# First mixture of experts: the weight splitting issued in pairs of pieces, six split slots, and a new order on ScalarE

## The chip, the core and the metric

The kernel runs on one core of a Trainium2 chip. The metric is the device time in microseconds (us) of one execution; the kernel before takes 2359.21 us, the median of 3 runs (2356.23 to 2360.47). Engines are named as the profile names them: PE is TensorE's matmul, PEld its weight load, DVE is VectorE, ACT is ScalarE, SP is the engine that issues the DMAs.

## The reference, cut to what matters

The program is a transformer block with a mixture of experts, followed by two more layers (a dense feed-forward in one, a second mixture in the other). All is float32, on 256 tokens of width 1024. The change is written in the first mixture, 16 experts, of which each token uses two:

```python
y = jnp.zeros_like(t)
for e in range(N_EXPERTS):
    he = jax.nn.silu(t @ w_gate[e]) * (t @ w_up[e])
    y = y + combine[:, e:e + 1] * (he @ w_down[e])
```

`w_gate` and `w_up` are 1024 x 512 for each expert, `w_down` is 512 x 1024: 6.29 MB of weights per expert, and no weight is read twice.

## The kernel before, in words

**Pieces.** All weights pass through one stream of numbered pieces of 128 x 1024 elements (0.5 MB). SP loads two at a time into `ring`, which has 12 slots (`RAW`). ScalarE copies a piece into `ring_hi`, rounded to the type that TensorE multiplies fast (`make_hi`, L421), and VectorE writes what the rounding lost into `ring_lo` (`make_lo`, L426). Both have 4 slots (`FINE`). TensorE multiplies with both parts and counts each piece it is done with on the semaphore `used` (called `pieces_used` on the chip).

**What holds what back.** `make_hi` of piece n waits until the piece has arrived and until `used` is at least n + 1 - FINE: the slot that it overwrites must be free. `make_lo` waits for the high part. A slot of `ring` is free for the next load when its low part is written.

**First mixture.** `stacked_experts` handles it, one expert per turn i of a loop that is written out 16 times. Expert i has 4 gate pieces, 4 up pieces, and in the same turn come the 4 down pieces of expert i - 1; in the stream their order is gate(i), up(i), down(i-1). TensorE's order in turn i is: gate(i) (L1506, L1507, 16 matmuls); turning the return table and folding the rows of expert i - 1 (L1543, L1554); up(i) (16 matmuls); a part of the gathering of later tokens (L1464); the scatter of four earlier experts into one quarter of the output (L1523); down(i-1) (16 matmuls). ScalarE's order and VectorE's order are in the two blocks below. ScalarE also copies gate rows (L1632), up rows (L1612), the return table (L1604, L1606), the gathered tokens (L1475, `xg`), the SiLU (L1616), the high part of the hidden rows (L1620), and the expert's output (L1600, `copy_output`). VectorE multiplies SiLU and up (L1662), makes the low part of the hidden rows (L1666), the low part of the output (L1671, `low_output`) and adds the scattered quarter to x (L1678, `add_to_x`).

**Second mixture.** 8 experts in 7 chunks each, by `sparse_experts`, with the same `make_hi`, `make_lo` and slots. Each piece is multiplied three ways (L442 to L444), so TensorE has 6 matmuls per piece. Once per expert, at its first chunk, the finished expert's output is scattered (L1240) and VectorE adds it to x in two instructions (L1375); TensorE may start the next down pieces only when both are done, since they go to the same banks. In VectorE's order these two stand behind the low parts of the first two down pieces, and those behind four up pieces, the low part of the output (`y_lo`, L1353), and four gate pieces.

Of the kernel before, what the change touches and what calls it, by code (L numbers as in the profile page):

```python
# [19 lines left out]
F32 = mybir.dt.float32  # L20
F32R = mybir.dt.float32r
BF16 = mybir.dt.bfloat16
ALU = mybir.AluOpType
ACT = mybir.ActivationFunctionType
# [118 lines left out]
class WeightStream:  # L143
# [1 line left out]

    RAW, FINE, AHEAD = 12, 4, 2

    def __init__(self):  # L150
        self.items, self.count = [], 0
# [14 lines left out]
def build(nc, ctx, A, consts_dram, const_cols, out):  # L166
# [29 lines left out]
    v, sc, pe = nc.vector, nc.scalar, nc.tensor  # L196
# [12 lines left out]
    ring = sb("ring", [P, WeightStream.RAW, 1024])  # L209
    ring_hi = sb("ring_hi", [P, WeightStream.FINE, 1024], dtype=F32R)  # L210
    ring_lo = sb("ring_lo", [P, WeightStream.FINE, 1024], dtype=F32R)
    x = sb("x", [P, HALVES, D])
# [12 lines left out]
    def bank(b, n=1):  # L225
        return psum[:, b * BANK:(b + n) * BANK]
# [170 lines left out]
    def raw_view(buf, slots, num, a, width):  # L397
        return buf[:, num[0] % slots, 0:a * width].rearrange("p (a n) -> p a n", a=a)
# [18 lines left out]
    def make_hi(e, num, a=2, width=FF):  # L417
        e.wait_ge(arrived[num[0] % RAW // 2], num[1] * 16 + 16 * (num[0] // RAW + 1))
        if not (isinstance(num[1], int) and num[0] + 12 * num[1] < FINE):
            e.wait_ge(used, count_after(num, 1 - FINE))  # L420
        sc.activation(raw_view(ring_hi, FINE, num, a, width), raw_view(ring, RAW, num, a, width), ACT.Copy) \  # L421
            .then_inc(hi_ready, 1)

    def make_lo(e, num, a=2, width=FF):
        e.wait_ge(hi_ready, count_after(num))
        v.tensor_tensor(raw_view(ring_lo, FINE, num, a, width), raw_view(ring, RAW, num, a, width),  # L426
                        raw_view(ring_hi, FINE, num, a, width).bitcast(F32), ALU.subtract).then_inc(lo_ready, 1)

    def make_his(e, pcs):
        for p in pcs:  # L430
# [964 lines left out]
    def stacked_experts(group, xn_split, disp, tag):  # L1395
# [15 lines left out]
        def gate_piece(i, q):  # L1411
            return group.n0 + q if i == 0 else group.n0 - 4 + 12 * i + q

        def up_piece(i, q):
            return gate_piece(i, q) + 4

        def down_piece(ex, j):
            return group.n0 + 16 + 12 * ex + j if ex < E - 1 else group.n0 - 4 + 12 * E + j

        def gathers(i):  # L1420
            return i + 1 < E
# [16 lines left out]
        def programs(st):  # L1438
# [157 lines left out]
            def scalar(e):  # L1596
                def copy_output(ex):
                    e.wait_ge(used, down_piece(ex, 3) + 1)
                    e.wait_ge(ret_ok, ex + 1)
                    sc.activation(y[0][ex % WIN], bank(3, 2), ACT.Copy, scale=weights[:, ex % WIN:ex % WIN + 1]).then_inc(y_out, 1)  # L1600

                def copy_return(ex):
                    e.wait_ge(ret_t, ex + 1)
                    sc.activation(both_sums[:], weight_sums(ex), ACT.Copy,  # L1604
                                  accum_out=weights[:, ex % WIN:ex % WIN + 1])
                    sc.copy(retT[:, ex % COPIES, :], bank(6)[:, E:E + SEQ]).then_inc(ret_ok, 1)  # L1606

                def copy_up(ex):
                    e.wait_ge(used, up_piece(ex, 3) + 1)
                    if ex:  # L1610
                        e.wait_ge(folded, ex)
                    sc.copy(u_sb[:], bank(1)).then_inc(u_out, 1)  # L1612

                def silu_of(ex):
                    e.wait_ge(folded, ex + 1)
                    sc.activation(s_g[:], gT, ACT.Silu).then_inc(silu, 1)  # L1616

                def high_hidden(ex):
                    e.wait_ge(hid, ex + 1)
                    sc.copy(hT[:, :, 0:SLOTS], hidden[:]).then_inc(hid_hi, 1)  # L1620

                for i in range(E):
                    for q in range(group.early if i == 0 else 0, 4):
                        make_hi(e, (gate_piece(i, q), 0))
                    if i > 1:
                        copy_output(i - 2)
                    for q in range(4):
                        make_hi(e, (up_piece(i, q), 0))
                    e.wait_ge(used, gate_piece(i, 3) + 1)
                    if i:  # L1630
                        e.wait_ge(folded, i)
                    sc.copy(g_sb[:], bank(0)).then_inc(g_out, 1)  # L1632
                    if i:
                        copy_return(i - 1)
                        silu_of(i - 1)
                        make_hi(e, (down_piece(i - 1, 0), 0), 1, 1024)
                        high_hidden(i - 1)
                        for j in range(1, 4):
                            make_hi(e, (down_piece(i - 1, j), 0), 1, 1024)
                    if gathers(i):  # L1640
                        for n in range(2):
                            first = min(i + 1, E - WIN)
                            e.wait_ge(gathered, 2 * i + n + 1)
                            copy_gathered(sc.copy, 2 * (i % 4) + n, first, bank(6 + n)).then_inc(xg_ok, 1)
                    copy_up(i)
                copy_output(E - 2)
                copy_return(E - 1)
                silu_of(E - 1)
                make_hi(e, (down_piece(E - 1, 0), 0), 1, 1024)
                high_hidden(E - 1)  # L1650
                for j in range(1, 4):
                    make_hi(e, (down_piece(E - 1, j), 0), 1, 1024)
                copy_output(E - 1)
                make_his(e, group.next)
                sc.preload_act_table_set(LOG_EXP)

            def vector(e):
# [20 lines left out]
                    v.tensor_tensor(to, to, bank(b), ALU.add).then_inc(added, 1)  # L1678

                for i in range(E):  # L1680
                    for q in range(group.early if i == 0 else 0, 4):
                        make_lo(e, (gate_piece(i, q), 0))
                    if i > 1:
                        low_output(i - 2)
                    if i > 2:
                        add_to_x(i - 3, scatter_plan[i - 1][0], 5)
                    for q in range(4):
                        make_lo(e, (up_piece(i, q), 0))
                    if i:
                        hidden_of(i - 1)  # L1690
                        make_lo(e, (down_piece(i - 1, 0), 0), 1, 1024)
                        low_hidden(i - 1)
                        for j in range(1, 4):
                            make_lo(e, (down_piece(i - 1, j), 0), 1, 1024)
                low_output(E - 2)
                add_to_x(E - 3, scatter_plan[E - 1][0], 5)
                hidden_of(E - 1)
                make_lo(e, (down_piece(E - 1, 0), 0), 1, 1024)
                low_hidden(E - 1)
                for j in range(1, 4):  # L1700
                    make_lo(e, (down_piece(E - 1, j), 0), 1, 1024)
                low_output(E - 1)
                for quarter in range(QUARTERS):
                    e.wait_ge(added, E - 2)
# [2013 lines left out]
```

## Time and profile before

| | |
|---|---|
| median of 3 runs | 2359.21 us |
| the profiled execution's own time | 2364.25 us |
| its span | 2362.1 us |
| busy PE / DVE / ACT | 95% / 78% / 65% |
| moved by DMA | 593.67 MB |
| first mixture, from its first to its last weight matmul | 290.7 to 574.8 us |
| second mixture | about 1322 to 2330 us |

A matmul of 512 columns is shown as about 390 ns, but the next one starts about 227 ns after it: matmuls are pipelined, and starts are what counts. The same holds for the instructions of DVE and ACT, which overlap by a little.

### The profile page before, as it was taken

How to read it: one execution, taken by the hardware profiler on the slowest of the kernel's cores; microseconds unless marked ns; L12 is line 12 of the kernel's file. 1: busy time of each engine (PE TensorE's matmuls, PEld its weight loads, DVE VectorE, ACT ScalarE, POOL GpSimd, SP SyncE). 2: the span in 40 equal slices, each digit the busy share in tenths (PEclk: the TensorE clock that was granted, in tenths of full speed). 3: DMA queues.
4: the chain of work that ended last, by engine and by line, in shares of the span. 5: the costliest groups of instructions: out<-in, count | busy, mean ns of one | idle time of the engine just before them, and what ended most of it. 6: DMA issues, size and time to landing. Idle time of an engine off the chain costs nothing. (4 is left out here: it accounts for less than half of the span.)

```text
span 2362.1 us, 35287 instructions
## 1 busy us (share of the span) xinstructions
PE 2242.1 (95%) x12323; PEld 1839.0 (78%) x12323; DVE 1846.9 (78%) x2017; ACT 1539.5 (65%) x2045; POOL 45.4 (2%) x56
## 2 busy tenths in 40 slices
PE   7989889999998999999989899999999999999997
PEld 6778567776776799987767688888888888888886
DVE  4655689997657656566667799999999999999995
ACT  4554389896544544455544587877777777777785
POOL 0000000000002000000003000000000000000000
PEclk9989999999989999999989999999999999999999
DMA  8434099997530355555500599999999999999892
GB/s 311 147 107 143 35 356 369 367 368 281 179 130 2 130 180 178 195 172 178 185 1 25 226 377 347 359 348 358 348 362 349 354 355 352 353 356 373 335 377 84
DMA packets 93735, 593.67 MB, mean 251 GB/s; under 512 B 17312, under 2 KB 20288, under 8 KB 22592
## 3 DMA queue, kind: packets, MB, share of 16 engines
q1 hardware_dynamic: 93632, 592.30, 67.1%
q8 instruction: 65, 1.06, 0.2%
q14 instruction: 38, 0.31, 0.0%
HBM read 591.21 MB, written 1.05 MB: 251 GB/s over the span
## 5 line engine op out<-in xcount | busy, mean ns | idle before, releaser
L426 DVE TENSOR_TENSOR ring_lo<-ring,ring_hi 128x1024 fp32r<-128x1024 f32 (+1 forms) x1120 | 1337.4, 1216 | 276.9 <-ACT ring_hi L421 215.9
L421 ACT ACTIVATE ring_hi<-ring 128x1024 fp32r<-128x1024 f32 (+1 forms) x1120 | 1162.5, 1056 | 410.8 <-PE psum L444 389.3
L442 PE MATMUL psum<-ring_hi,xg_hi 128*128 128x512 f32 x896 | 354.3, 395 | 3.7 <-DVE ring_lo L426 2.4
L444 PE MATMUL psum<-ring_hi,xg_lo 128*128 128x512 f32 x896 | 349.6, 390 | 0.0
L443 PE MATMUL psum<-ring_lo,xg_hi 128*128 128x512 f32 x896 | 348.9, 389 | 0.0
L442 PE MATMUL psum<-ring_hi,xT_hi 128*128 128x512 f32 (+2 forms) x512 | 200.7, 392 | 14.0 <-DVE ring_lo L426 6.1
L442 PEld LDWEIGHTS psum<-ring_hi,xg_hi 128*128 128x128 f32 x896 | 168.3, 188 | 37.7 <-DVE ring_lo L426 2.9
L443 PE MATMUL psum<-ring_lo,xT_hi 128*128 128x512 f32 (+2 forms) x512 | 197.3, 385 | 0.0
L444 PE MATMUL psum<-ring_hi,xT_lo 128*128 128x512 f32 (+2 forms) x512 | 197.1, 385 | 0.0
L444 PEld LDWEIGHTS psum<-ring_hi,xg_lo 128*128 128x128 f32 x896 | 168.2, 188 | 35.7
L443 PEld LDWEIGHTS psum<-ring_lo,xg_hi 128*128 128x128 f32 x896 | 168.5, 188 | 33.4
L442 PE MATMUL psum<-ring_hi,hT_hi 128*128 128x512 f32 x448 | 176.1, 393 | 8.0 <-DVE x L1375 5.6
L444 PE MATMUL psum<-ring_hi,hT_lo 128*128 128x512 f32 x448 | 174.5, 390 | 0.0
L443 PE MATMUL psum<-ring_lo,hT_hi 128*128 128x512 f32 x448 | 174.4, 389 | 0.0
L442 PE MATMUL psum<-xT_hi,ring_hi 128*128 128x256 f32 x480 | 136.1, 284 | 2.6 <-DVE xT_lo L1838 1.6
L444 PE MATMUL psum<-xT_hi,ring_lo 128*128 128x256 f32 x480 | 135.9, 283 | 0.0
L443 PE MATMUL psum<-xT_lo,ring_hi 128*128 128x256 f32 x480 | 135.9, 283 | 0.0
L442 PEld LDWEIGHTS psum<-ring_hi,xT_hi 128*128 128x128 f32 x512 | 98.3, 192 | 36.4 <-issue 9.2
L1506 PE MATMUL psum<-ring_hi,xg 128*128 128x512 f32 x256 | 112.7, 440 | 8.6 <-DVE ring_lo L426 6.4
L444 PEld LDWEIGHTS psum<-ring_hi,xT_lo 128*128 128x128 f32 x512 | 98.3, 192 | 19.3
L443 PEld LDWEIGHTS psum<-ring_lo,xT_hi 128*128 128x128 f32 x512 | 98.5, 192 | 17.8
L442 PEld LDWEIGHTS psum<-ring_hi,hT_hi 128*128 128x128 f32 x448 | 84.1, 188 | 28.4 <-issue 9.6
(549 smaller groups left out, 3227.8 us busy)
## 6 DMA issues: line engine op xcount, KB each, us to landing
ring<-in_moe_w_gate_dram SPq DMA_DIRECT2D x112, 1024.0 KB, 4.8
ring<-in_moe_w_up_dram SPq DMA_DIRECT2D x112, 1024.0 KB, 4.8
ring<-in_moe_w_down_dram SPq DMA_DIRECT2D x112, 1024.0 KB, 4.7
ring<-in_w_in_dram SPq DMA_DIRECT2D x38, 1024.0 KB, 5.6
ring<-in_w_gate_dram SPq DMA_DIRECT2D x32, 1024.0 KB, 6.9
ring<-in_w_up_dram SPq DMA_DIRECT2D x32, 1024.0 KB, 7.2
ring<-in_w_down_dram SPq DMA_DIRECT2D x32, 1024.0 KB, 7.1
ring<-in_ffn_w_gate_dram SPq DMA_DIRECT2D x14, 1024.0 KB, 4.8
```

The costliest lines, as they stand in the source:

```text
L421: sc.activation(raw_view(ring_hi, FINE, num, a, width), raw_view(ring, RAW, num, a, width), ACT.Copy) \
L426: v.tensor_tensor(raw_view(ring_lo, FINE, num, a, width), raw_view(ring, RAW, num, a, width), raw_view(ring_hi, FINE, num, a, width).bitca ...
L442: pe.matmul(out_, lhsT[0], rhs[0], start=start, stop=False)
L443: pe.matmul(out_, lhsT[0], rhs[1], start=False, stop=False)
L444: return pe.matmul(out_, lhsT[1], rhs[0], start=False, stop=stop)
L1506: pe.matmul(to, lhsT, w[0], start=start, stop=False)
```

## The change

Five things are changed. `FINE` goes from 4 to 6, for the whole program. In the first mixture `make_hi` and `make_lo` are replaced by versions that treat two pieces in one instruction of 2048 columns; the high version waits for `used` to be at least n + 2 - FINE, where n is the first piece of the pair, the low one for both high parts. On ScalarE the four gate pieces of expert i + 1 are moved from the head of turn i + 1 to turn i: the first pair ahead of the token copies, the second between them and the copy of the up rows. The first pair of down pieces moves ahead of the copy of the gate rows. And the size of a scratch buffer is set to 1024 bytes, which makes room for the two more slots.

```diff
-    RAW, FINE, AHEAD = 12, 4, 2
+    RAW, FINE, AHEAD = 12, 6, 2
...
+    def pair_view(buf, slots, n):
+
+        return buf[:, n % slots:n % slots + 2, :].rearrange("p m x -> p (m x)")
+
+    def make_hi_pair(e, n):
+        e.wait_ge(arrived[n % RAW // 2], 16 * (n // RAW + 1))
+        e.wait_ge(used, n + 2 - FINE)
+        sc.activation(pair_view(ring_hi, FINE, n), pair_view(ring, RAW, n), ACT.Copy).then_inc(hi_ready, 2)
+
+    def make_lo_pair(e, n):
+        e.wait_ge(hi_ready, n + 2)
+        v.tensor_tensor(pair_view(ring_lo, FINE, n), pair_view(ring, RAW, n), pair_view(ring_hi, FINE, n).bitcast(F32),
+                        ALU.subtract).then_inc(lo_ready, 2)
...
+                for q in range(group.early, 4, 2):
+                    make_hi_pair(e, gate_piece(0, q))
                 for i in range(E):
-                    for q in range(group.early if i == 0 else 0, 4):
-                        make_hi(e, (gate_piece(i, q), 0))
                     if i > 1:
                         copy_output(i - 2)
-                    for q in range(4):
-                        make_hi(e, (up_piece(i, q), 0))
+                    for q in range(0, 4, 2):
+                        make_hi_pair(e, up_piece(i, q))
+                    if i:
+                        make_hi_pair(e, down_piece(i - 1, 0))
                     e.wait_ge(used, gate_piece(i, 3) + 1)
...
                     if i:
                         copy_return(i - 1)
                         silu_of(i - 1)
-                        make_hi(e, (down_piece(i - 1, 0), 0), 1, 1024)
                         high_hidden(i - 1)
-                        for j in range(1, 4):
-                            make_hi(e, (down_piece(i - 1, j), 0), 1, 1024)
+                        make_hi_pair(e, down_piece(i - 1, 2))
                     if gathers(i):
+                        make_hi_pair(e, gate_piece(i + 1, 0))
                         for n in range(2):
...
                             copy_gathered(sc.copy, 2 * (i % 4) + n, first, bank(6 + n)).then_inc(xg_ok, 1)
+                        make_hi_pair(e, gate_piece(i + 1, 2))
                     copy_up(i)
...
-    nc = _bacc.Bacc("TRN2", target_bir_lowering=False, num_devices=1)
+    nc = _bacc.Bacc("TRN2", target_bir_lowering=False, num_devices=1,
+                    dynamic_dma_scratch_size=1024)
```

On VectorE the loops over single pieces become loops over pairs; the order is kept. Line numbers of the changed kernel are 14 to 16 higher there (`make_hi_pair` is L436, `make_lo_pair` L440).

ScalarE in the first mixture, before, from one expert's output copy to the gate pieces of the next expert (`L421` is `make_hi`, `L1475` the token copies, `L1612` the up rows):

```order
L1600 ACTIVATE y_rows<-psum,slot_weights 128x1024
L421 ACTIVATE ring_hi<-ring 128x1024 x4
L1632 COPY gate_rows<-psum 128x512
L1604 ACTIVATE weight_parts,slot_weights<-psum 128x2
L1606 CAST return_pT<-psum 128x256
L1616 ACTIVATE silu_gT<-psum 128x256
L421 ACTIVATE ring_hi<-ring 128x1024
L1620 CAST hT<-hiddenT 128x4x64
L421 ACTIVATE ring_hi<-ring 128x1024 x3
L1475 CAST xg<-psum 128x2x4x64 x2
L1612 COPY up_rows<-psum 128x512
L421 ACTIVATE ring_hi<-ring 128x1024 x4
```

The same stretch of ScalarE in the changed kernel (`L436` is `make_hi_pair`, `L1489` the token copies, `L1626` the up rows):

```order
L1614 ACTIVATE y_rows<-psum,slot_weights 128x1024
L436 ACTIVATE ring_hi<-ring 128x2048 x3
L1648 COPY gate_rows<-psum 128x512
L1618 ACTIVATE weight_parts,slot_weights<-psum 128x2
L1620 CAST return_pT<-psum 128x256
L1630 ACTIVATE silu_gT<-psum 128x256
L1634 CAST hT<-hiddenT 128x4x64
L436 ACTIVATE ring_hi<-ring 128x2048 x2
L1489 CAST xg<-psum 128x2x4x64 x2
L436 ACTIVATE ring_hi<-ring 128x2048
L1626 COPY up_rows<-psum 128x512
```

The group of three is up, up, down; of the group of two the second is the first gate pair of the next expert, and the single one after the token copies is its second gate pair. In the kernel before all four gate pieces of the next expert stand behind the up rows.

VectorE in the first mixture, before, one turn from the low part of an output to the next gate pieces:

```order
L1671 SCALAR_TENSOR_TENSOR xT_lo<-psum,slot_weights,y_rows 128x1024
L1678 TENSOR_TENSOR x<-x,psum 128x512
L426 TENSOR_TENSOR ring_lo<-ring,ring_hi 128x1024 x4
L1662 TENSOR_TENSOR hiddenT<-silu_gT,psum 128x256
L426 TENSOR_TENSOR ring_lo<-ring,ring_hi 128x1024
L1666 TENSOR_TENSOR hT<-hiddenT,hT 128x4x64
L426 TENSOR_TENSOR ring_lo<-ring,ring_hi 128x1024 x7
```

The same turn of VectorE in the changed kernel:

```order
L1686 SCALAR_TENSOR_TENSOR xT_lo<-psum,slot_weights,y_rows 128x1024
L1693 TENSOR_TENSOR x<-x,psum 128x512
L440 TENSOR_TENSOR ring_lo<-ring,ring_hi 128x2048 x2
L1677 TENSOR_TENSOR hiddenT<-silu_gT,psum 128x256
L440 TENSOR_TENSOR ring_lo<-ring,ring_hi 128x2048
L1681 TENSOR_TENSOR hT<-hiddenT,hT 128x4x64
L440 TENSOR_TENSOR ring_lo<-ring,ring_hi 128x2048 x3
```

Nothing changes place on VectorE but one thing: the low part of the second down piece is now made together with the first, ahead of the low part of the hidden rows. TensorE's order and that of the DMA issues are the same as before.

## Rows read from the trace of the kernel before

**Rows 1.** Windows: stretch, length, busy by engine, PE clock, DMA share, GB/s.

```profile
375.00:545.00 170.00, 170.00 (x837) 131.89 (x836) 161.10 (x160) 155.13 (x229) 0.00 (x0) 1.00 0.96 369
1380.00:2322.00 942.00, 933.10 (x4327) 773.88 (x4325) 870.14 (x804) 735.10 (x765) 0.00 (x0) 1.00 0.92 353
```

**Rows 2.** Timeline, DVE, one turn: start, length, engine, line, operation, count.

```profile
424.44 4.63 DVE L426 TENSOR_TENSOR ring_lo<-ring,ring_hi 128x1024 fp32r<-128x1024 f32 x4 [0.87 <-ACT ring_hi L421]
...
430.78 4.62 DVE L426 TENSOR_TENSOR ring_lo<-ring,ring_hi 128x1024 fp32r<-128x1024 f32 x4
...
437.17 3.50 DVE L426 TENSOR_TENSOR ring_lo<-ring,ring_hi 128x1024 fp32r<-128x1024 f32 x3
441.58 1.23 DVE L426 TENSOR_TENSOR ring_lo<-ring,ring_hi 128x1024 fp32r<-128x1024 f32 x1 [0.92 <-ACT ring_hi L421]
```

**Rows 3.** Timeline, ACT, the same turn.

```profile
435.77 0.41 ACT L1620 CAST hT<-hiddenT 128x256 fp32r<-128x256 f32 x1 [0.89 <-DVE hiddenT L1662]
436.08 2.95 ACT L421 ACTIVATE ring_hi<-ring 128x1024 fp32r<-128x1024 f32 x3
438.94 1.17 ACT L1475 CAST xg<-psum 128x384 fp32r<-128x384 f32 x4
439.98 0.62 ACT L1612 COPY up_rows<-psum 128x512 f32<-128x512 f32 x1
440.46 1.10 ACT L421 ACTIVATE ring_hi<-ring 128x1024 fp32r<-128x1024 f32 x1
```

**Rows 4.** Waits, 300 to 550 us: total, times, longest.

```profile
PEld psum L1506 <- DVE ring_lo L426: 24.0, 69, 0.4
DVE ring_lo L426 <- ACT ring_hi L421: 18.1, 18, 4.4
```

**Rows 5.** Groups by shape, 276 to 281 us: busy, mean ns.

```profile
L3459 DVE TENSOR_TENSOR xn_moe_lo<-xn_rows,xn_moe_hi 128x2048 fp32r<-128x2048 f32 x1 | 2.3, 2293 | 0.8 <-DVEq L193 0.8
L3454 ACT CAST xn_moe_hi<-xn_rows 128x2048 fp32r<-128x2048 f32 x1 | 1.9, 1881 | 0.0
```

**Rows 6.** Timeline, PE, one turn, and the start of expert 1.

```profile
304.32 0.77 PE L1506 MATMUL psum<-ring_hi,xg 128*128 128x512 f32 x1 [3.61 <-DVE ring_lo L426]
...
430.16 0.65 PE L1543 MATMUL psum<-consts,dispatch 128*128 128x144 f32 x4
...
432.35 0.48 PE L1506 MATMUL psum<-ring_hi,xg 128*128 128x512 f32 x1
...
439.27 0.39 PE L1506 MATMUL psum<-ring_hi,hT 128*128 128x512 f32 x1
...
442.68 0.39 PE L1507 MATMUL psum<-ring_lo,hT 128*128 128x512 f32 x1
...
444.00 0.50 PE L1506 MATMUL psum<-ring_hi,xg 128*128 128x512 f32 x1
444.33 0.40 PE L1507 MATMUL psum<-ring_lo,xg 128*128 128x512 f32 x1
```

**Rows 7.** Timeline, second mixture, ACT, DVE and PE where an expert changes.

```profile
1461.35 1.01 ACT L1299 ACTIVATE y_hi<-psum 128x1024 fp32r<-128x1024 f32 x1
...
1462.83 1.22 DVE L1353 TENSOR_TENSOR y_lo<-psum,y_hi 128x1024 fp32r<-128x1024 f32 x1
...
1471.48 1.28 DVE L1375 SCALAR_TENSOR_TENSOR x<-psum,comb,x 128x1024 f32<-128x1024 f32 x1
1473.07 1.28 DVE L1375 SCALAR_TENSOR_TENSOR x<-psum,comb,x 128x1024 f32<-128x1024 f32 x1 [0.31 <-DVE x L1375]
...
1473.35 0.39 PE L444 MATMUL psum<-ring_hi,xg_lo 128*128 128x512 f32 x1
1474.48 0.49 PE L442 MATMUL psum<-ring_hi,hT_hi 128*128 128x512 f32 x1 [0.75 <-DVE x L1375]
```

**Rows 8.** Waits of PE, whole span.

```profile
PE psum L442 <- DVE ring_lo L426: 11.7, 8, 4.3
PE psum L442 <- DVE x L1375: 5.6, 7, 1.2
```

More of the change, by code:

```diff
@@ L1648, in scalar @@
                 silu_of(E - 1)
-                make_hi(e, (down_piece(E - 1, 0), 0), 1, 1024)
+                make_hi_pair(e, down_piece(E - 1, 0))
                 high_hidden(E - 1)
-                for j in range(1, 4):
-                    make_hi(e, (down_piece(E - 1, j), 0), 1, 1024)
+                make_hi_pair(e, down_piece(E - 1, 2))
                 copy_output(E - 1)
@@ L1680, in vector @@
                 for i in range(E):
-                    for q in range(group.early if i == 0 else 0, 4):
-                        make_lo(e, (gate_piece(i, q), 0))
+                    for q in range(group.early if i == 0 else 0, 4, 2):
+                        make_lo_pair(e, gate_piece(i, q))
                     if i > 1:
@@ L1686, in vector @@
                         add_to_x(i - 3, scatter_plan[i - 1][0], 5)
-                    for q in range(4):
-                        make_lo(e, (up_piece(i, q), 0))
+                    for q in range(0, 4, 2):
+                        make_lo_pair(e, up_piece(i, q))
                     if i:
                         hidden_of(i - 1)
-                        make_lo(e, (down_piece(i - 1, 0), 0), 1, 1024)
+                        make_lo_pair(e, down_piece(i - 1, 0))
                         low_hidden(i - 1)
-                        for j in range(1, 4):
-                            make_lo(e, (down_piece(i - 1, j), 0), 1, 1024)
+                        make_lo_pair(e, down_piece(i - 1, 2))
                 low_output(E - 2)
@@ L1697, in vector @@
                 hidden_of(E - 1)
-                make_lo(e, (down_piece(E - 1, 0), 0), 1, 1024)
+                make_lo_pair(e, down_piece(E - 1, 0))
                 low_hidden(E - 1)
-                for j in range(1, 4):
-                    make_lo(e, (down_piece(E - 1, j), 0), 1, 1024)
+                make_lo_pair(e, down_piece(E - 1, 2))
                 low_output(E - 1)
```

## The prediction

> **What bounds the kernel now.** I read the page's slices first, to find the stretches where DMA and the engines are busiest, then windows for each stage, then the timeline of one turn engine by engine, and the waits last. The reader should see three things.
>
> First, in the first mixture nobody has much room. TensorE is shown busy throughout, VectorE 161.10 of 170 us, ScalarE 155.13, and DMA stands at a share of 0.96 [rows 1]. One expert takes 441.58 - 424.44 = 17.14 us [rows 2]. VectorE idles once a turn, 0.9 us, and waits there for ScalarE's high part of the next expert's first gate piece [rows 2]. ScalarE is late with it because it does the high parts of three down pieces, the token copies and the up rows first, back to back from 436.08 [rows 3]. So the turn is a ring of ScalarE and VectorE: the hidden rows on VectorE release ScalarE at 435.77, and 440.46 + 1.10 = 441.56 releases VectorE again. TensorE waits in small bits for low parts, 69 times, 24.0 us as PEld counts them [rows 4].
>
> Second, the second mixture is bound by TensorE (933.10 of 942 us, DMA share 0.92) [rows 1]. What TensorE loses there is the wait for the addition to x, 7 times, 5.6 us in all [rows 8].
>
> Third, outside the mixtures TensorE's waits for low parts come to 11.7 us over the whole span, the longest 4.3 [rows 8].
>
> **The change part by part, first mixture.** Pairs save the fixed part of an instruction. Low parts of single pieces start (4.63 - 1.23) / 3 = 1.13 us apart [rows 2]; an instruction of 2048 columns of the same kind takes 2.29 us alone [rows 5], less the overlap of 0.1 that the singles show (1.23 - 1.13) it is 2.19 a pair. That is 0.07 a pair, about 0.45 us a turn on VectorE. On ScalarE singles start (2.95 - 1.10) / 2 = 0.925 apart [rows 3] and a pair takes 1.88, 1.78 after overlap [rows 5]: 0.07 a pair, again 0.45 a turn. With the idle time gone VectorE alone would turn in 17.14 - 0.92 - 0.45 = 15.8 us. DMA, at a share of 0.96 now, would be full at 17.14 x 0.96 = 16.5.
>
> But a pair asks for two free slots. The second gate pair of expert i + 1 must wait until `used` reaches n - 4, and counted back through the stream that is the second down piece of turn i. It is a new chain, and it runs through all three engines. With P the start of TensorE's first down matmul:
> - two down pieces, 8 matmuls 0.227 apart ((442.68 - 439.27) / 15) and 0.39 for the last: 7 x 0.227 + 0.39 = 1.98 [rows 6];
> - ScalarE's pair 1.88 and VectorE's pair 2.29 [rows 5], and three handoffs at 0.04 (441.58 comes 0.02 after ScalarE's end [rows 2, 3]), 0.12: TensorE gets the second gate pair at P + 6.27, while it would be ready for it at about P + 5.6 (24 matmuls and one restart);
> - gate pieces 2 and 3: 8 matmuls, the first step 0.33 after a wait (444.33 - 444.00), 1.94; then turning and folding 432.35 - 430.16 = 2.19 [rows 6]: the up matmuls start at P + 10.4;
> - from the first up matmul to the next P the trace has 439.27 - 432.35 = 6.92, with two small waits in it [rows 6]. With pairs only one wait can be there: the second up pair is written at 6.23 + 1.71 (from the end of the gate parts, 424.44 + 4.63, to 430.78) + 2.19 + 2.29 = P + 12.4 [rows 2, 5], and TensorE wants it at P + 12.3. I take 6.8.
>
> Sum: 6.27 + 4.13 + 6.8 = 17.2 us a turn, against 17.14. The stall of VectorE moves from the first gate piece to the second gate pair and grows to about 1.4 us, which eats what the pairs save. ScalarE meets its other dates: the first gate pair needs all up pieces used (about P + 14.6) and is ready by P + 17, before VectorE wants it at P + 17.5. So the 12 turns in the steady state are worth +0.06 x 12 = +0.7. Without the small up wait the turn is 17.0 (-2 over the 12); with handoffs of 0.1 and a full 6.92 it is 17.5 (+4).
>
> The first turns are not steady. TensorE waits 3.61 us for expert 1's gate pieces today [rows 6]. The first pair of them now comes early, but the second still stands behind the token copies, and expert 0's up pieces come in pairs, one step of 1.1 later. I walked these turns the same way and find TensorE 2 us ahead by the fourth. Bounds: all 3.6 of that wait, or 1 us lost (the coarser step alone). Taken: -2. The last turns keep their order. First mixture together: -1, between -6 and +5.
>
> **Six slots elsewhere.** ScalarE may now be two more pieces ahead of TensorE. In a steady TensorE-bound stage that is worth nothing. It is worth something where VectorE falls behind for a moment: where an expert of the second mixture changes. There VectorE's order is four gate parts, `y_lo`, four up parts, the low hidden rows, two down parts, then the two additions. The second addition ends at 1473.07 + 1.28 = 1474.35, and TensorE, whose matmul before started at 1473.35, would have gone on at 1473.58: it restarts at 1474.48 with a step longer by 0.1, so 1.0 us are lost [rows 7]. What holds VectorE back is how late it enters this passage, since until then each low part follows a high part that waits for a slot. With two pieces more, of 6 matmuls each, it would be up to 12 x 0.227 = 2.7 us ahead, except that `y_hi` on ScalarE has to wait for the last down piece: it starts at 1461.35 because another high part stands before it, and could start at 1460.4 [rows 7]. That puts `y_lo` at 1461.45 instead of 1462.83, the additions 1.0 us or more earlier, and TensorE no longer waits. The first of the 7 waits (the longest, 1.2 [rows 8]) comes where VectorE is held by something else, and stays. Gain: 5.6 - 1.2 = 4.4, and 6 x 0.1 for restarts, 5.0. Bounds: 0 (the additions come no earlier) and 6.3 (all seven).
>
> Of the 11.7 us of waits for low parts [rows 8] the longest, 4.3, is set by the order of the code, not by slots: ScalarE and VectorE do a norm there before more pieces. (The wait of 3.6 us counted above is under another line of the matmuls and not among them.) What I can tie to slots is where low parts waited for high parts that waited for TensorE in the two input projections. Taken: -2, between 0 and -5. The scratch size costs nothing: no queue but SP's moves this kernel's data.
>
> Sum: -1 - 5 - 2 = -8. The profiled execution took 2364.25 (span 2362.1), 5.0 above the median of the runs; 2364.25 - 8 = 2356.2 in its terms, 2351 in those of the runs.
>
> **The rivals.**
> - A: the new chain does not close, VectorE turns at its own pace and DMA sets the end at 16.5 us a turn. For it: VectorE's one idle wait today [rows 4] is the one that the new order removes. Against it: `used` needs the second down piece, as counted above. It gives 12 x (17.2 - 16.5) = 8 more: 2343. The Trainium skill speaks for this case (VectorE: DVE Perf Modes, the section on the TRN2 errata): the latency of SBUF is paid between instructions, so fewer and larger ones are faster. By that rule alone the mixture gains; the trace has the same saving, but VectorE's time is not what closes my chain.
> - B: nothing comes of the slots. The additions to x are still late, for VectorE is busy without a gap from the gate parts on, and the first mixture is even. For it: the first of the seven waits is of that kind. It gives -1 to -2: 2358.
> - C, slower: TensorE's one wait of 0.7 us and more in each turn, in place of many small ones, lets its clock fall. Place: the second gate pair. For it: after the wait of 3.61 us the next matmul took 0.77 us instead of 0.39, as at the lower of the clock's two levels, 1.2 against 2.4 GHz [rows 6]. Against it: waits of 0.75 in the second mixture are followed by 0.49 and then full speed [rows 7], at a granted clock of 1.00 [rows 1]. If it happens, and the 8 matmuls of the two gate pieces then take a step of 0.454 instead of 0.227, that is 1.8 us for each of 12 turns, 22, less 8 of the forecast's gains: 2359 + 14 = 2373. It decides from 0.7 us lost a turn, where 12 x 0.7 outweighs those 8. The chain at its long end, 17.5, falls short of that point by itself.
>
> **How the numbers follow.** Forecast 0.55 (its own range 2346 to 2356), A 0.15, B 0.19, C 0.11. Below 0.2% (4.7 us) this measurement can't tell a change from none. Faster than 2354.5: nine tenths of the forecast less the weak end of its bounds, say 0.44, and A, 0.15, together 0.59. Same: the rest of the forecast, 0.11, B, 0.18, together 0.29. Slower: C and a little of B, 0.12. The range reaches from A's lower side, 2341, to 2362, just beyond B, and leaves C out.
>
> **What would show it.** In the changed profile the turn of the first mixture is 17.0 to 17.4 us; VectorE waits once a turn, before the second gate pair, for ScalarE, which itself waits there for TensorE's down matmuls; TensorE has one wait of about 0.7 us between the second and third gate piece. If instead VectorE has no such wait and the turn is near 16.5 with a DMA share of 1, A is right. In the second mixture the waits for the addition to x should be 1 or 2 instead of 7; 7 again is B. Matmuls twice as long inside the steady turns are C. I am wrong altogether if the turn is longer than 17.5 at full clock, or if a stage that I gave nothing moves by more than 3 us.

## The result, and the profile after

| | before | after |
|---|---|---|
| median | 2359.21 us | 2346.76 us (2341.73 to 2348.26, 5 runs) |
| ratio | | 0.9937, 95% interval 0.9919 to 0.9955 |
| profiled execution, its span | 2364.25, 2362.1 us | 2341.73, 2339.6 us |

The change is worth 12.4 us; a second run of it on another chip gave 0.9938 (0.9924 to 0.9951). The forecast was 2351, 8 us faster. But the gain doesn't come from the first mixture, for which most of the change is written.

Windows of the changed kernel, the stretches that answer to [rows 1] (columns as there; the second is shifted by 10 us, since the second mixture starts earlier):

```profile
375.00:545.00 170.00, 161.40 (x819) 132.57 (x818) 153.61 (x98) 148.13 (x165) 0.00 (x0) 1.00 0.96 364
1370.00:2312.00 942.00, 935.31 (x4340) 777.73 (x4339) 840.67 (x810) 715.01 (x774) 0.00 (x0) 1.00 0.92 350
```

In the first mixture TensorE is now busy 161.40 of 170 us, where it was 170.00, and less is moved per second, 364 GB/s against 369. In the second mixture it is busy for 2.2 us more in the same length: more of the work lies in the window.

VectorE, one turn of the changed kernel, from one second gate pair to the next:

```profile
418.17 2.29 DVE L440 TENSOR_TENSOR ring_lo<-ring,ring_hi 128x2048 fp32r<-128x2048 f32 x1 [1.64 <-ACT ring_hi L436]
...
429.44 4.49 DVE L440 TENSOR_TENSOR ring_lo<-ring,ring_hi 128x2048 fp32r<-128x2048 f32 x2
435.57 2.29 DVE L440 TENSOR_TENSOR ring_lo<-ring,ring_hi 128x2048 fp32r<-128x2048 f32 x1 [1.64 <-ACT ring_hi L436]
```

435.57 - 418.17 = 17.40 us a turn, against 17.14 [rows 2]. The idle time of 0.92 us before the first gate piece has become one of 1.64 before the second gate pair. ScalarE in the same turn says why:

```profile
427.02 0.41 ACT L1634 CAST hT<-hiddenT 128x256 fp32r<-128x256 f32 x1 [0.78 <-DVE hiddenT L1677]
427.33 3.72 ACT L436 ACTIVATE ring_hi<-ring 128x2048 fp32r<-128x2048 f32 x2
430.96 1.17 ACT L1489 CAST xg<-psum 128x384 fp32r<-128x384 f32 x4
433.55 1.92 ACT L436 ACTIVATE ring_hi<-ring 128x2048 fp32r<-128x2048 f32 x1 [1.43 <-PE psum L1521]
435.37 0.57 ACT L1626 COPY up_rows<-psum 128x512 f32<-128x512 f32 x1
```

It is no longer late with its own work, as in [rows 3]: it stands idle for 1.43 us behind the token copies and waits for TensorE (`PE psum L1521`, a weight matmul) to be done with a slot. TensorE, from the first down matmul to the next turn's:

```profile
431.45 0.39 PE L1520 MATMUL psum<-ring_hi,hT 128*128 128x512 f32 x1
...
436.67 0.39 PE L1521 MATMUL psum<-ring_lo,xg 128*128 128x512 f32 x1
437.92 0.50 PE L1520 MATMUL psum<-ring_hi,xg 128*128 128x512 f32 x1 [0.86 <-DVE ring_lo L440]
438.25 0.39 PE L1521 MATMUL psum<-ring_lo,xg 128*128 128x512 f32 x1
...
442.06 0.48 PE L1520 MATMUL psum<-ring_hi,xg 128*128 128x512 f32 x1
...
448.85 0.39 PE L1520 MATMUL psum<-ring_hi,hT 128*128 128x512 f32 x1
```

So the loop is closed: with P = 431.45, ScalarE starts the pair at P + 2.10, VectorE at P + 4.12, TensorE at P + 6.47. The waits of the stretch 300 to 550 us, next to [rows 4]:

```profile
PEld psum L1520 <- DVE ring_lo L440: 24.9, 29, 2.5
DVE ring_lo L440 <- ACT ring_hi L436: 21.3, 14, 2.7
ACT ring_hi L436 <- PE psum L1521: 18.1, 13, 1.7
```

About as much is waited on low parts, 24.9 us against 24.0, but in 29 pieces, not 69. The third row is the chain's: ScalarE waits for TensorE 13 times, once a turn, where the same wait of the kernel before (`ACT ring_hi L421 <- PE psum L1507`) came 3 times and to 2.0 us.

The pairs themselves are as long as [rows 5] had it, by the groups of the page (busy, mean ns, idle before):

```profile
L440 DVE TENSOR_TENSOR ring_lo<-ring,ring_hi 128x2048 fp32r<-128x2048 f32 x95 | 214.7, 2289 | 31.1 <-ACT ring_hi L436 31.0
L436 ACT ACTIVATE ring_hi<-ring 128x2048 fp32r<-128x2048 f32 x95 | 176.9, 1913 | 19.4 <-PE psum L1521 18.1
```

In the second mixture the timeline where an expert changes answers to [rows 7], ScalarE, VectorE and TensorE:

```profile
1444.63 1.03 ACT L1313 ACTIVATE y_hi<-psum 128x1024 fp32r<-128x1024 f32 x1 [1.66 <-PE psum L458]
```

```profile
1445.69 1.22 DVE L1367 TENSOR_TENSOR y_lo<-psum,y_hi 128x1024 fp32r<-128x1024 f32 x1
...
1456.29 1.28 DVE L1389 SCALAR_TENSOR_TENSOR x<-psum,comb,x 128x1024 f32<-128x1024 f32 x1 [0.31 <-DVE x L1389]
```

```profile
1457.60 0.39 PE L458 MATMUL psum<-ring_hi,xg_lo 128*128 128x512 f32 x1
1457.83 0.40 PE L456 MATMUL psum<-ring_hi,hT_hi 128*128 128x512 f32 x1
```

ScalarE now stands ready for `y_hi` and waits 1.66 us for TensorE. The second addition ends at 1457.57, before TensorE's last gate or up matmul starts, and the down matmuls go on at the normal step of 0.23. Waits of PE over the whole span, for [rows 8]:

```profile
PE psum L456 <- DVE ring_lo L426: 10.1, 7, 4.7
PE psum L456 <- DVE x L1389: 1.2, 1, 1.2
```

**Where the time went.** The program has the same 12,323 matmuls before and after, so their starts can be laid side by side, one by one. Against the first profile of before that gave -8.1 us ahead of the first mixture, where nothing but the number of slots is changed. A second profile of the kernel before, taken for this reason (`b_again`, below), is itself 7.3 us earlier there. Against that one, the steps are:

| us, after minus before | changed kernel | its second profile |
|---|---|---|
| up to the first mixture | -0.7 | +0.3 |
| its start, to expert 3's turn | +0.1 | -0.1 |
| from there to the down matmuls of the last turn | +2.1 | +2.1 |
| its end | -0.3 | -0.7 |
| input projections of the two layers | -1.9, -2.1 | -1.9, -2.4 |
| second mixture | -7.2 | -7.3 |
| sum of these rows | -10.0 | -10.0 |
| all other stretches | -5.2 | +0.8 |
| whole span | -15.2 | -9.2 |

From the first mixture on the rows agree within 0.4 us between the two profiles of the changed kernel, and the sum of the other stretches does not. Their largest steps lie where the granted clock differs. Ahead of the first mixture, the first and the second profile of before:

```profile
0.00:283.00 283.00, 247.77 (x1297) 202.15 (x1298) 166.18 (x252) 131.98 (x217) 0.20 (x4) 0.96 0.43 150
0.00:283.00 283.00, 243.90 (x1331) 200.70 (x1331) 167.95 (x256) 135.35 (x225) 0.20 (x4) 0.98 0.42 150
```

And between 1125 and 1260 us, the second profile of before and the first of the changed kernel:

```profile
1125.00:1260.00 135.00, 123.41 (x1092) 93.99 (x1089) 93.17 (x150) 57.88 (x152) 20.01 (x22) 0.89 0.19 67
1125.00:1260.00 135.00, 123.72 (x1119) 93.46 (x1118) 92.79 (x148) 58.64 (x157) 21.64 (x25) 0.94 0.18 62
```

A granted clock lower by 0.02 over 283 us is worth 5.7 us of TensorE's time, one lower by 0.05 over 135 us 6.8 (both my estimates, from clocks rounded to hundredths): against 7.3 and 5.4 found. The second of these steps comes in both profiles of the changed kernel (5.4 and 4.5 us, each at 0.94), though the forecast gave that stretch nothing; slots alone gain 1.8 us there, and the kernel that keeps the rule of four slots outside 2.9, while the two profiles of before are even. It goes the other way too: between 680 and 780 us the second profile of the changed kernel has a clock of 0.84 against 0.89, and loses 5.7 us, the first loses 1.4.

### The profile page after: what moved, and what is told of

It reads as the page before. It is cut to its first block and busy times, and to the rows that moved or that the text cites. A ratio compares the mean times of both kernels' runs of the same rounds, so it can differ in the third digit from the quotient of the medians.

```text
span 2339.6 us, 35162 instructions
## 1 busy us (share of the span) xinstructions
PE 2216.9 (95%) x12323; PEld 1834.3 (78%) x12323; DVE 1803.2 (77%) x1922; ACT 1498.2 (64%) x1950; POOL 45.4 (2%) x56
## 3 DMA queue, kind: packets, MB, share of 16 engines
HBM read 591.21 MB, written 1.05 MB: 253 GB/s over the span
## 5 line engine op out<-in xcount | busy, mean ns | idle before, releaser
L426 DVE TENSOR_TENSOR ring_lo<-ring,ring_hi 128x1024 fp32r<-128x1024 f32 (+1 forms) x930 | 1073.4, 1212 | 144.6 <-ACT ring_hi L421 137.9
L421 ACT ACTIVATE ring_hi<-ring 128x1024 fp32r<-128x1024 f32 (+1 forms) x930 | 936.0, 1051 | 178.1 <-PE psum L458 147.7
L440 DVE TENSOR_TENSOR ring_lo<-ring,ring_hi 128x2048 fp32r<-128x2048 f32 x95 | 214.7, 2289 | 31.1 <-ACT ring_hi L436 31.0
L436 ACT ACTIVATE ring_hi<-ring 128x2048 fp32r<-128x2048 f32 x95 | 176.9, 1913 | 19.4 <-PE psum L1521 18.1
L1520 PE MATMUL psum<-ring_hi,xg 128*128 128x512 f32 x256 | 107.1, 418 | 17.9 <-DVE ring_lo L440 14.9
```

Source lines behind the costliest of these rows:

```text
L436: sc.activation(pair_view(ring_hi, FINE, n), pair_view(ring, RAW, n), ACT.Copy).then_inc(hi_ready, 2)
L440: v.tensor_tensor(pair_view(ring_lo, FINE, n), pair_view(ring, RAW, n), pair_view(ring_hi, FINE, n).bitcast(F32), ALU.subtract).then_inc(l ...
L1520: pe.matmul(to, lhsT, w[0], start=start, stop=False)
```

## The experiments

In the order of their questions. All ratios are to the kernel before, timed on the same chip; "turn" is read from VectorE's timeline near 430 us.

| kernel | slots | order on ScalarE | pieces | turn, us | ratio (95%) |
|---|---|---|---|---|---|
| before | 4 | old | single | 17.14 | 1 |
| `e1_six_slots` | 6 | old | single | 17.14 | 0.9929 (0.9913 to 0.9945) |
| `e2_four_slot_rule_outside` | 6 in the mixture | new | pairs | 17.40 | 0.9992 (0.9984 to 1.0001) |
| after, `after_again` | 6 | new | pairs | 17.40 | 0.9937, 0.9938 |
| `e6_old_order_pairs` | 6 | old | pairs | 17.67 | 1.0001 (0.9988 to 1.0014) |
| `e5_new_order_four_slots` | 4 in the mixture | new | single | 18.56 | 1.0005 (0.9996 to 1.0015) |
| `e3_second_gate_pair_single`, `e3_again` | 6 | new | pairs but one | 16.14 | 0.9884, 0.9862 |
| `e4_new_order_single_pieces`, `e4_again` | 6 | new | single | 16.08 | 0.9856, 0.9861 |
| `e7_only_gates_moved` | 6 | only the gates moved | single | 16.46 | 0.9882 (0.9864 to 0.9900) |
| `e8_scratch_only` | 4 | old | single | 17.15 | 0.9997 (0.9989 to 1.0006) |

**Slots alone** (with the scratch size of 1024 bytes, as in the changed kernel).

```diff
-    RAW, FINE, AHEAD = 12, 4, 2
+    RAW, FINE, AHEAD = 12, 6, 2
```

> The kernel before with FINE = 6 and the small scratch buffer, and nothing else: single pieces, the old order on ScalarE. Theory 1 (the gain lies outside the first mixture and comes from the slots): the turns of the first mixture stay near 17.14 us, since their ring runs through ScalarE's own order and not through free slots; the seven waits for the addition to x shrink to one (-6.8 us in the changed kernel's trace) and the two input projections give the 4 us that they gave there; sum -11, ratio 0.995. Rival (the edits of the first mixture carry the gain): ratio 1.000, and seven waits for the addition remain.

Measured: 2344.89 us (2337.32 to 2348.46), at least as fast as the whole change. The old ring of the first mixture stands as it was:

```profile
436.13 4.63 DVE L426 TENSOR_TENSOR ring_lo<-ring,ring_hi 128x1024 fp32r<-128x1024 f32 x4 [0.92 <-ACT ring_hi L421]
...
453.29 4.63 DVE L426 TENSOR_TENSOR ring_lo<-ring,ring_hi 128x1024 fp32r<-128x1024 f32 x4 [0.92 <-ACT ring_hi L421]
```

and the wait for x falls as in the changed kernel:

```profile
PE psum L442 <- DVE x L1375: 1.2, 1, 1.2
```

**The slots taken out again, outside the first mixture.** In the changed kernel `make_hi` alone goes back to the rule of four slots:

```diff
-        if not (isinstance(num[1], int) and num[0] + 12 * num[1] < FINE):
-            e.wait_ge(used, count_after(num, 1 - FINE))
+        if not (isinstance(num[1], int) and num[0] + 12 * num[1] < 4):
+            e.wait_ge(used, count_after(num, 1 - 4))
```

> The changed kernel, but make_hi outside the pairs waits as if there were four slots (used at least n - 3); pairs, order and memory as changed. Theory 1: second mixture and input projections go back to what they were before (seven waits for the addition to x), the first mixture keeps its turn of 17.40 us and is about 1 us slower in all than before; ratio 1.000 (+1 us), unless the clock gives something. Rival (the first mixture carries the gain): the ratio stays near 0.994.

Measured: 2358.38 us, no gain left, and the seven waits are back:

```profile
PE psum L456 <- DVE x L1389: 5.6, 7, 1.2
```

These two runs show that the change's gain is the two slots outside the first mixture. What is written for the first mixture brings nothing as it stands.

**The suspected chain, cut at one place.** In the changed kernel the second gate pair of the next expert is split by single instructions; all other pairs stay.

```diff
-                        make_hi_pair(e, gate_piece(i + 1, 2))
+                        for q in (2, 3):
+                            make_hi(e, (gate_piece(i + 1, q), 0))
```

(and the same two pieces on VectorE).

> The changed kernel with the second gate pair of each next expert split as two single pieces on ScalarE and VectorE, in the same place. Theory 2 (the turn is set by the chain TensorE's two down pieces, ScalarE's pair, VectorE's pair, TensorE's gate pieces 2 and 3): a single piece needs one down piece used and 1.06 + 1.22 us instead of 1.91 + 2.29, so it is ready at about P + 3.4 and its fellow at P + 4.7, before TensorE wants them at P + 5.4 and 6.3. VectorE's idle time before them goes, and the turn falls from 17.40 to 16.5 (DMA full) or 16.2 (what TensorE's own work adds up to): -0.9 x 12 = -11 us against the changed kernel, ratio to before 0.989. Rival (something else sets the turn, such as the low up pair or DMA): the turn stays between 17.2 and 17.4.

> The changed kernel with only the second gate pair as two single pieces, a second time. Chain theory: turn 16.1 again, ratio 0.986 to 0.990, some 10 to 14 us faster than the changed kernel on the same chip (12 turns by 1.26 us, less or more by the start).

Measured: 2332.12 and 2329.85 us, 15 us below the changed kernel's 2345.19 on the chip of the second run. One pair in six set the turn. ScalarE and VectorE in the first of these runs:

```profile
438.85 1.17 ACT L1489 CAST xg<-psum 128x256 fp32r<-128x256 f32 x4
440.22 2.01 ACT L421 ACTIVATE ring_hi<-ring 128x1024 fp32r<-128x1024 f32 x2 [0.20 <-PE psum L1521]
```

```profile
429.76 4.49 DVE L440 TENSOR_TENSOR ring_lo<-ring,ring_hi 128x2048 fp32r<-128x2048 f32 x2
434.46 0.42 DVE L1678 TENSOR_TENSOR hiddenT<-silu_gT,psum 128x256 f32<-128x256 f32 x1 [0.21 <-ACT silu_gT L1630]
...
445.90 4.49 DVE L440 TENSOR_TENSOR ring_lo<-ring,ring_hi 128x2048 fp32r<-128x2048 f32 x2
```

Its first down matmul is at 439.05, so ScalarE starts piece 2 at P + 1.17 (one down piece used) where the pair had to wait until P + 2.10, and its wait of 1.43 us shrinks to 0.20. VectorE's wait of 1.64 us is gone. The windows row of the second run:

```profile
375.00:545.00 170.00, 169.01 (x880) 143.08 (x879) 163.66 (x114) 155.79 (x187) 0.00 (x0) 1.00 0.99 390
```

**No pairs at all.** The order and slots of the changed kernel, every pair done by two single instructions with the single waits:

```diff
-        e.wait_ge(arrived[n % RAW // 2], 16 * (n // RAW + 1))
-        e.wait_ge(used, n + 2 - FINE)
-        sc.activation(pair_view(ring_hi, FINE, n), pair_view(ring, RAW, n), ACT.Copy).then_inc(hi_ready, 2)
+        for m in range(2):
+            make_hi(e, (n + m, 0))
```

(and `make_lo_pair` in the same way with two `make_lo`).

> The changed kernel with its order and six slots, but all pieces split one by one. It tells order from pairs. Theory 2: without pairs no chain of 17.4 closes; VectorE needs 17.14 - 0.92 = 16.2 us and DMA 16.5, so the turn is 16.5 and the kernel 11 us faster than the changed one, ratio 0.989: the pairs are then what costs, and their saving of 0.45 us per turn on VectorE is worth nothing. Rival (pairs are needed, the fixed part of an instruction counts): the turn is 17.1 to 17.4, ratio 0.994 or above.

> The changed kernel's order and six slots with single pieces, a second time, on one chip with the two others. If it differs from the kernel with only the second gate pair split by more than the measurement, its ratio is again 0.984 to 0.987; the ledger of the traces gives it no advantage (turns 16.08 against 16.14), so a difference of 0.3% would be the early part of the program and its clock, and may vanish.

Measured: 2326.97 and 2328.83 us, the fastest version, 16 to 20 us below the changed kernel. The 0.3% between it and the kernel with five pairs did not come back (0.9861 and 0.9862 on one chip), so the other pairs cost nothing and save nothing that the time shows. Their saving is there on VectorE, 163.66 us busy in the row above against 166.89 in the row below, but TensorE is busy 169.01 of 170 us in both, and it sets the turn of 16.1 us. The windows row without pairs (first run):

```profile
375.00:545.00 170.00, 169.01 (x882) 143.23 (x881) 166.89 (x168) 159.48 (x240) 0.00 (x0) 1.00 0.98 389
```

**Is it the order, or the slots?** The same kernel with the rule of four slots in the first mixture only:

```diff
-        for m in range(2):
-            make_hi(e, (n + m, 0))
+        for k in (n, n + 1):
+            e.wait_ge(used, k + 1 - 4)
+            make_hi(e, (k, 0))
```

> The changed kernel's order on ScalarE, all pieces single, six slots in the rest of the program, but in the first mixture a high part waits for used as with four slots. It asks whether the new order needs the two slots. Slot theory: with four slots the gate pieces 0 and 1 of the next expert wait for down pieces 0 and 1 of the turn (1.1 and 2.0 us after P, TensorE's first down matmul), the token copies stand behind them and slip, and the turn is 16.6 to 17.1 us instead of the 16.08 of the same kernel with six: ratio 0.989 to 0.993. Order theory: the order alone frees VectorE, the turn is 16.1 and the ratio is 0.986 again. The second mixture gains 6 to 7 us and layer 1's input projections 2 in both.

Measured: 2362.81 us, turn 18.56. Worse than either theory: the order without the slots costs 15.2 us over eleven turns, from expert 3's on. I had counted the gate pieces' wait (1.56 us) and the tokens behind it, but not the down pair ahead of the gate rows, which waits 0.68 us for the up matmuls and holds back the SiLU, and with it the hidden rows:

```profile
434.62 2.06 ACT L421 ACTIVATE ring_hi<-ring 128x1024 fp32r<-128x1024 f32 x2 [0.68 <-PE psum L1520]
436.59 0.56 ACT L1647 COPY gate_rows<-psum 128x512 f32<-128x512 f32 x1
...
442.23 2.01 ACT L421 ACTIVATE ring_hi<-ring 128x1024 fp32r<-128x1024 f32 x2 [1.56 <-PE psum L1520]
444.15 1.17 ACT L1488 CAST xg<-psum 128x384 fp32r<-128x384 f32 x4
```

TensorE then waits once for the hidden rows and once for the tokens in that turn.

**Pairs in the old order**, with six slots: the gate pairs behind the up rows, the first down pair behind the SiLU (both loops as in the kernel before, with the pair versions).

```diff
-                    if i:
-                        make_hi_pair(e, down_piece(i - 1, 0))
                     e.wait_ge(used, gate_piece(i, 3) + 1)
...
                         silu_of(i - 1)
+                        make_hi_pair(e, down_piece(i - 1, 0))
                         high_hidden(i - 1)
```

> The changed kernel's pairs and six slots, but ScalarE in the old order of the first mixture: the gate pieces of the next expert behind the up rows, the first down pair behind the SiLU. Chain theory: the second gate pair still needs the second down piece used, P + 2.0, and ScalarE (down pair, token copies, up rows, first gate pair) is free for it at about the same time, so the turn stays at 17.3 to 17.6 us and the ratio is 0.993 to 0.996. Rival, the order was the mistake and pairs alone are good: the turn falls to 16.6 to 16.9, ratio 0.988 to 0.991. Rival, the order was needed by the pairs: ScalarE then closes the old ring with whole pairs, and the turn is 17.8 or more, ratio 0.997 or above.

Measured: 2359.38 us. The ratio is that of the second rival (the order was needed by the pairs), and the turn, 17.67, lies between the chain theory's 17.6 and that rival's 17.8. The mechanism is the rival's as well: VectorE does not wait at the second gate pair. It waits 0.67 us at the first, which ScalarE starts when its own work is done, at 443.36, back to back with the up rows. That is the old ring of [rows 3] with whole pairs in it. VectorE has a second wait there, of 1.16 us, for the first down pair, which stands behind the SiLU on ScalarE again:

```profile
439.96 2.29 DVE L440 TENSOR_TENSOR ring_lo<-ring,ring_hi 128x2048 fp32r<-128x2048 f32 x1 [1.16 <-ACT ring_hi L436]
```

ScalarE in that turn:

```profile
439.73 0.42 ACT L1634 CAST hT<-hiddenT 128x256 fp32r<-128x256 f32 x1
440.02 1.95 ACT L436 ACTIVATE ring_hi<-ring 128x2048 fp32r<-128x2048 f32 x1
441.84 1.21 ACT L1489 CAST xg<-psum 128x384 fp32r<-128x384 f32 x4
442.88 0.66 ACT L1626 COPY up_rows<-psum 128x512 f32<-128x512 f32 x1
443.36 3.92 ACT L436 ACTIVATE ring_hi<-ring 128x2048 fp32r<-128x2048 f32 x2
```

The chain theory's ratio missed above all because the start turns cost 7.0 us here by the ledger (expert 1's first gate pair is waited for 5.59 us, before 3.61); the turns from expert 3's to the last one's down matmuls cost 6.4. With the new order the pairs start without a loss, 0.1.

**Only the gate pieces moved**, single pieces, six slots, the down pieces where they were.

> The kernel before with six slots and single pieces, and of the new order only one move: the gate pieces of the next expert ahead of the token copies and the up rows. The down pieces keep their old places. Theory: the old ring (hidden rows on VectorE, three down pieces, tokens and up rows on ScalarE, first gate piece, VectorE) is opened by this move alone, VectorE runs without its 0.92 us gap, TensorE's own work sets the turn at 16.1 to 16.2 us, and the ratio is 0.985 to 0.987. Rival, the down pair ahead of the gate rows is needed too (its high part is early, so the hidden rows come sooner): the turn stays above 16.5 and the ratio above 0.989.

Measured: 2332.73 us, turn 16.46, between the two expectations. The move of the gates is worth 17.14 - 16.46 = 0.68 us a turn, that of the down pair another 0.38; in time the two kernels differ by 0.17% (2328.83 of the full order on the same chip) with overlapping intervals, so only the turns show the down pair's part.

**The scratch size alone.**

```diff
-    nc = _bacc.Bacc("TRN2", target_bir_lowering=False, num_devices=1)
+    nc = _bacc.Bacc("TRN2", target_bir_lowering=False, num_devices=1,
+                    dynamic_dma_scratch_size=1024)
```

> The kernel before with the scratch buffer's size set to 1024 bytes and nothing else. Theory (the forecast gave it nothing): ratio 1.000 within 0.001, the ledger of TensorE's matmuls flat. Rival: what the two traces leave unexplained, 3 to 4 us that every variant with six slots is ahead of the sum of its steps, comes from this size; then the ratio is 0.998 to 0.9988. If it is flat, that remainder belongs to the profile of before that the ledger is counted from, which ran 4 us under the median of its runs.

Measured: 2360.05 against 2360.44 us, nothing.

**Both kernels once more.**

> The kernel before, profiled once more, to see what of the ledger between the two profiled executions was the execution and not the kernel. If the 8 us by which the changed kernel was ahead before the first mixture were the execution's, this profile has a span near 2357 and is ahead of the first profile by 4 to 7 us at the same place; if they were the change's, the span is 2362 again and it is ahead by less than 1. Steady turn of 17.14, seven waits for the addition to x in both.

> The changed kernel, a second time, to have its time and its ledger on the same chip as the best versions. Turn 17.40, seven of the eight expert changes without the wait for x, ratio 0.992 to 0.996. What is left of its lead of 8 us before the first mixture over the first profile of before should be under 2 us against the second profile of before.

Measured: before 2356.89 us in its one execution, span 2354.8, 7.3 us earlier at the first mixture than the first profile. From there on the distance stays the same, but for a passing 1.9 us at the mixture's end, and is 7.4 at the last matmul. After: 2345.19 us, and +0.3 at the first mixture. So the first profile of before had lost those 7.3 us ahead of the first mixture, at a lower granted clock and without any edit. The second one lies 4 us under the median of the runs beside it (2360.93), which is part of why a variant's median is better against theirs than its ledger is against this profile.

## Why the prediction was right, and where it was not

**The chain of the first mixture: right, in each link.** Forecast and measured: ScalarE starts the second gate pair at P + 2.02, measured 2.10; TensorE gets it at P + 6.27, measured 6.47 (the pair on ScalarE 1.92 instead of 1.88, its handoff to VectorE 0.10 instead of 0.04); from there to the up matmuls 4.13, measured 442.06 - 437.92 = 4.14; from there to the next P 6.8, measured 6.79. Sum 17.2, measured 17.40, so that a turn lost 0.26 us where 0.06 was forecast. That the chain sets the turn was shown by cutting it: 16.14 us.

**The start turns: wrong.** I took -2 and found 0. Expert 1's first gate pair does come early, but TensorE then waits for the tokens (0.81 us) and for the second pair, which stands behind the token copies:

```profile
296.29 0.50 PE L1520 MATMUL psum<-ring_hi,xg 128*128 128x512 f32 x1 [0.81 <-ACT xg L1489]
...
300.49 0.50 PE L1520 MATMUL psum<-ring_hi,xg 128*128 128x512 f32 x1 [2.07 <-DVE ring_lo L440]
```

and for the hidden rows of expert 0, 1.16 us. With single pieces the same order takes 4.5 us from these turns (2.8 and 1.7), so the pairs give that away as well. First mixture together: -1 forecast, about +2 found, within the bounds.

**Six slots in the second mixture: right, and 2 us too small.** The mechanism is in the rows above, and the runs with slots alone and without them bracket it. The term was 6 changes of 0.83 us, 5.0. In the ledger seven changes step down, by 0.9 to 1.05 each, 6.9 and 7.0 in the two profiles; the stage from its first to its last weight matmul gives 7.2 and 7.3. The view of waits names x seven times, of which the first stays; the seventh change, near 2212 us, loses the same and is not named there. And the loss at each is the 1.0 that I had worked out in [rows 7], not the 0.73 of the waits.

**The input projections: right in place, half in size.** -2 forecast, -1.9 in one layer and -2.1 in the other, 4.0 in all, gone in the kernel that keeps the rule of four slots outside. TensorE's waits for low parts say the same: 0.59 and 0.82 us in the first layer before and none after, 2.44 in the second before and 0.38 after (of the two waits behind it, one grows from 0.22 to 0.83 and one of 0.81 is new, since the matmuls between them no longer run at the lower clock).

**The sum: near, and in part by luck.** By the ledger the terms are about +2 - 4 - 7.2 = -9, and the forecast was -8. That they meet is partly luck: the first mixture came out 3 us worse than its term, the other two terms together 4 us better. The medians differ by more, 12.4 and 14.6 us. The forecast had nothing for the rest of 3 to 5, and its size fits the granted clock. On the chip of the second run, the runs of before have a mean granted clock of 0.9797 over their span (9 runs), those of the changed kernel 0.9818 (5 runs). Among the recorded runs of before alone, a clock higher by 0.001 goes with a time shorter by 1.3 us; if all of the time followed TensorE's clock it would be 2.4. The 0.0021 are then worth 3 to 5 us, an estimate. Span times granted clock, which takes the clock out by the second measure, gives 2310.1 us before and 2301.0 after, 9.1 less, as the ledger has it. Why the changed kernel has the higher clock stays open. One place can be seen: in the second layer's input projection, where TensorE's wait for a low part shrank from 2.44 to 0.38 us, the clock from 1110 to 1130 us is 1.00 instead of 0.91, with slots alone as well, and 0.91 again with the rule of four slots outside. But that last kernel has a higher clock over its span too (0.9811 against 0.9794 on its chip), while the one with the scratch size alone has not (0.9793 against 0.9796).

The prediction also says that it is wrong altogether if a stage that it gave nothing moves by more than 3 us. By the ledger one did: between 1125 and 1260 us both profiles gain, 5.4 and 4.5 us, at a higher granted clock; from 680 to 780 us the second one loses 5.7, at a lower one. The chain and the slots do what was forecast, but the sum has no term for the granted clock, and with it the gain is larger than forecast. How much of the clock's part belongs to the change and how much to the single execution is not shown.

**The rivals.** C fell: TensorE's one wait of 0.86 us a turn is followed by a step of 0.33 and then 0.23 at a granted clock of 1.00. B fell with the one remaining wait of seven. A did not happen, since the chain closed. But its limit was wrong too, and there my prediction reasoned badly: I took the DMA share of 0.96 for a floor of 16.5 us a turn, and the kernel with the chain cut ran at 16.14 with 390 GB/s.

**Pairs as such.** I priced the saving rightly, 0.07 us a pair (4.49 for two pairs, 4.63 for four single ones). The Trainium skill (VectorE: DVE Perf Modes, the section on the TRN2 errata) has fewer and larger instructions faster, and for the instruction the trace agrees, by that 0.07 us; for the kernel it does not hold here: the larger instruction also waits for the later of its two slots and hands over the first piece later, and this one place costs 17.40 - 16.14 = 1.26 us a turn.

## What to carry to other kernels

Before merging two instructions that each wait for a free buffer, count for each pair which consumer step frees its later buffer, and close the loop through all engines: one pair out of six set the turn here, while the other five were free. When a change has several parts, time the plainest one by itself: two more slots alone gave all of this change's gain, and the new order with them, without the pairs, gave more than twice as much. An order that runs a producer further ahead needs the buffers for it: with four slots the same order took 18.56 us a turn, against 17.14 of the old one.

## What was not expected of the hardware

- The DMA share is no measure of what is left. Before it was 0.96 at 369 GB/s, and that looked like 4% of room; with other work out of the way the same transfers ran at 389 and 390 GB/s at shares of 0.98 and 0.99, 5.7% more.
- Two profiles of one and the same kernel differed by 7.3 us in the first 283 us, at granted clocks of 0.96 and 0.98, and hardly after. A ledger against a single profile would have put those down to the change. Setting the granted clock beside each stretch shows which steps may be the execution's.
